# Four pieces of 272 tokens instead of 384 + 352 + 352 in the up-projection of a feed-forward part

## The chip, the core and the metric
The kernel runs on one core of one Trainium2 chip. The metric is device time in microseconds (us) of one execution. The engines are TensorE (PE for its matmuls and PEld for its weight loads in the rows), VectorE (DVE), ScalarE (ACT), GpSimd (POOL) and SyncE (SP, which issues DMAs here). Each runs its own queue in order, and they meet at semaphores only.

## What is computed
One layer of a decoder trunk for 1024 prompt tokens and 8 samples of 8 tokens, 1088 tokens in all. The layer is a three-branch mixer, then a feed-forward part with a causal convolution of width 3 between its two projections, then a final norm. The change lies in the feed-forward part:

```python
x = x + merged @ w_out
u = rmsnorm(x, norm_ffn) @ w_up                      # 1024 -> 2 * 2816 columns
ext = jnp.concatenate([conv_buf.astype(dt), u], axis=1)
c = conv_b + sum(conv_w[i] * ext[:, i:i + T] for i in range(CONV_WIDTH))
gate, val = jnp.split(c, 2, axis=-1)
x = x + (jax.nn.silu(gate) * val) @ w_down
...
y_prompt = rmsnorm(xp, norm_final)
```

## The kernel before
`stage_out_ffn` is the last stage. Activations lie with features on the 128 partitions and the 1088 tokens along the free axis. The work is a list of 92 **units**, numbered n. A unit is one block of 128 output features for all tokens: 8 units "out" (the mixer's output projection), then four parts of the feed-forward part. Each part has "up" units, two for each of its blocks of 128 gated features (h = 0 the gate, h = 1 the value), and then 8 "down" units that add the part's share to x. The parts have 12, 12, 12 and 8 up units, 44 in all; the last part has its down units twice, for two groups of tokens. So the kind of unit goes from up to down four times and from down to up three times, always at an even n.

The matmuls keep more precision than one pass gives: weights and activations are each split into a high and a low half, and every product is three matmuls, low half of x by high weights (L135), high by high (L136), high by low (L137). Each matmul loads its own 128 x 128 weights. A unit runs over its pieces of tokens (`CH`, 384 + 352 + 352), and within a piece over the 8 blocks k of the contraction. So an up unit is 3 pieces x 8 x 3 = 72 matmuls, and 1088 x 24 columns stream through the array.

A piece takes one PSUM bank of 512 fp32 numbers. Of the eight banks even units take 0 to 2 and odd ones 3 to 5; banks 6 and 7 serve sums over partitions (`sums`, L2615) and transposes. PE starts unit n when its weights are split (`ws`) and unit n - 2 has been read out of PSUM (`ev` at least n - 1), which `ready` says. Per unit the others do this:

- SP loads the weights of the unit into the one buffer fu_wt once the previous ones are split.
- VectorE, when unit n's matmuls are done, reads the bank out (L2849 with the norm's factor for an up unit, in pieces of 384, 352 and 288 and then the 64 sample tokens in L2850; L2783 for out and down units), makes the high half of the weights of unit n + 2 (fu_wh, L124), and for an up unit does the convolution (L2857, L2860, L2863) and, after h = 1, the gating (L2867, L2870).
- GpSimd makes the low half of the weights (fu_wl, L129), which releases PE and SP, and the low half of the gated activations (fu_al, L129). ScalarE does the sigmoid and the high half fu_ah.

The first two down units of a part are interleaved: both go over all but the last block of the contraction, since that block's activations come late, and then each does its last block, waiting for `al`. The third down unit needs weights that VectorE only starts after the first has been read out.

The first up unit (n = 8) takes its input while it is still being made: ScalarE writes the high half mh and VectorE the low half ml in 3 x 8 steps (L2790), piece by piece of `CH`, and PE waits before each (piece, k) for that step (`xl`). Behind unit 8 PE does `sums`. VectorE turns them into a mean (L2797, `mean` goes to 3), ScalarE takes the root, and VectorE the reciprocal (L2799). Only then can it read out unit 8, and only after that make the weights of unit 10.

Of the kernel before, what the change touches and what calls it, by code (L numbers as in the profile page):

```python
# [24 lines left out]
KT = D // P  # L25
SEQ, NB, NQ = 1024, 8, 8
TS = NB * NQ
# [20 lines left out]
CH = ((0, 384), (384, 352), (736, 352))  # L48
# [83 lines left out]
def product(nc, out, w, x, start, stop):  # L132

    (wh, wl), (xh, xl) = ((t.bitcast(F32R) for t in pair) for pair in (w, x))
    nc.tensor.matmul(out, wh, xl, start=start, stop=False)  # L135
    nc.tensor.matmul(out, wh, xh, start=False, stop=False)  # L136
    return nc.tensor.matmul(out, wl, xh, start=False, stop=stop)  # L137
# [20 lines left out]
def build(nc, a, outs, scratch):  # L158

    with ExitStack() as ctx:  # L160
# [16 lines left out]
        with tensor("o", [P, 6, T]) as g.branches:  # L177
# [29 lines left out]
            with tensor("mh", [P, KT, T]) as mh, tensor("ml", [P, KT, T]) as ml:  # L207
                with semaphores(g):
                    stage_merge(g, mh, ml)
                with tensor("x1", [P, KT, T]) as x1:  # L210
                    with semaphores(g):
                        stage_out_ffn(g, mh, ml, x1)
# [2239 lines left out]
def stage_out_ffn(g, mh, ml, x1):  # L2452
# [4 lines left out]
    nc, a, V_ = g.nc, g.a, g.nc.vector  # L2457
# [4 lines left out]
    samp = lambda t, o: t[:, S0:EXT].rearrange("p (b q) -> p b q", q=NQ + 2)[:, :, o:o + NQ]  # L2462
# [5 lines left out]
    u, cv = work[:, 0:2, :], work[:, 2:4, :]  # L2468
# [5 lines left out]
    L = len(parts) - 1  # L2474
    units = [("out", 0, t, 0) for t in range(KT)]
# [8 lines left out]
    GROUPS = (((0, 384), (384, 384)), ((768, 320),))  # L2484
    cols = (slice(0, 768), slice(768, T))
    blocks = (range(0, 6), range(6, NJ))
    chunks = lambda n: GROUPS[units[n][3]] if units[n][:2] == ("down", L) else CH

    with ExitStack() as ctx:
        sb = lambda name, shape, dt=F32: ctx.enter_context(nc.sbuf_tensor(f"fu_{name}", shape, dt))  # L2490
# [2 lines left out]
        wl, wh = sb("wl", [P, 2, KT, P]), sb("wh", [P, 2, KT, P])  # L2493
# [13 lines left out]
        s = {n: g.sem(f"fu_{n}") for n in names}  # L2507
# [11 lines left out]
        with nc.Block() as block:  # L2519
# [61 lines left out]
            def _(eng):  # L2581
                def dense(n, c, c0, m, ks, xh, xl, first, last):
                    for k in ks:
                        mm = product(nc, g.ps[:, 3 * (n % 2) + c, 0:m], (wh[:, n % 2, k, :], wl[:, n % 2, k, :]),
                                     (xh[:, k, c0:c0 + m], xl[:, k, c0:c0 + m]), first and k == ks[0], last and k == ks[-1])
                    return mm

                def ready(n):
                    eng.wait_ge(s["ws"], n + 1)
                    if n >= 2:  # L2590
                        eng.wait_ge(s["ev"], n - 1)

                def full(n):
                    ready(n)
                    for c, (c0, m) in enumerate(CH):
                        for k in range(KT):
                            if n == KT:
                                eng.wait_ge(s["xl"], KT * c + k + 1)
                            mm = dense(n, c, c0, m, [k], mh, ml, k == 0, k == KT - 1)
                    mm.then_inc(s["mm"], 1)  # L2600

                def down(n, ks, first, last):
                    for k in ks:
                        eng.wait_ge(s["al"], parts[units[n][1]][0] + k + 1)
                        for c, (c0, m) in enumerate(chunks(n)):
                            mm = dense(n, c, c0, m, [k], ah, al, first and k == 0, last and k == ks[-1])
                    if last:
                        mm.then_inc(s["mm"], 1)
# [44 lines left out]
                for n, (kind, i, t, h) in enumerate(units):  # L2653
                    if kind != "down":
                        full(n)
                        if n == KT:
                            sums()
                        continue
                    nj = parts[i][1]
                    if t == 0 and h == 0:  # L2660
                        ready(n)
                        down(n, range(nj - 1), True, False)
                        ready(n + 1)
                        down(n + 1, range(nj - 1), True, False)
                        down(n, [nj - 1], False, True)
                        down(n + 1, [nj - 1], False, True)
                    elif t >= 2 or h:
                        ready(n)
                        down(n, range(nj), True, True)
# [102 lines left out]
            def _(eng):  # L2772
                def weights(n):
                    if n < NUM:
                        eng.wait_ge(s["w"], 16 * (n + 1))
                        if n >= 2:
                            eng.wait_ge(s["mm"], n - 1)
                        high(eng, wh[:, n % 2, 0:width(n)], wt[:, 0:width(n)]).then_inc(s["wh"], 1)
# [62 lines left out]
                def up(n, i, j, h):  # L2841
                    eng.wait_ge(s["mm"], n + 1)
                    if j:
                        eng.wait_ge(s["co"], 2 * j + h - 1)
                        eng.wait_ge(s["m"] if h == 0 else s["cv"], j if h == 0 else 2 * j)
                    b0 = 3 * (n % 2)
                    for c, (c0, m) in enumerate(CH):
                        m = min(m, SEQ - c0)
                        V_.tensor_tensor(u[:, h, 2 + c0:2 + c0 + m], g.ps[:, b0 + c, 0:m], inv[:, c0:c0 + m], ALU.mult)  # L2849
                    V_.tensor_tensor(samp(u[:, h], 2), g.ps[:, b0 + 2, m:m + TS].rearrange("p (b q) -> p b q", q=NQ),  # L2850
                                     inv[:, SEQ:T].rearrange("p (b q) -> p b q", q=NQ), ALU.mult).then_inc(s["ev"], 1)
                    weights(n + 2)
                    eng.wait_ge(s["ev"], n + 1)
                    eng.wait_ge(s["st"], 2 * j + h + 1)
                    if j:
                        eng.wait_ge(s["act"] if h == 0 else s["al"], j)
                    V_.tensor_scalar(cv[:, h, 0:E], u[:, h, 0:E], column(g.cw[:, 0], h, j), column(g.cb, h, j),  # L2857
                                     ALU.mult, ALU.add).then_inc(s["t0"], 1)
                    eng.wait_ge(s["t0"], 2 * j + h + 1)
                    V_.scalar_tensor_tensor(out=cv[:, h, 0:E], in0=u[:, h, 1:1 + E], scalar=column(g.cw[:, 1], h, j),  # L2860
                                            in1=cv[:, h, 0:E], op0=ALU.mult, op1=ALU.add).then_inc(s["t1"], 1)
                    eng.wait_ge(s["t1"], 2 * j + h + 1)
                    V_.scalar_tensor_tensor(out=cv[:, h, 0:E], in0=u[:, h, 2:2 + E], scalar=column(g.cw[:, 2], h, j),  # L2863
                                            in1=cv[:, h, 0:E], op0=ALU.mult, op1=ALU.add).then_inc(s["cv"], 1)
                    if h:
                        eng.wait_ge(s["sg"], j + 1)
                        V_.tensor_tensor(cv[:, 0, 0:E], sg, cv[:, 0, 0:E], ALU.mult).then_inc(s["m"], 1)  # L2867
                        eng.wait_ge(s["m"], j + 1)
                        eng.wait_ge(s["cv"], 2 * j + 2)
                        V_.tensor_tensor(act[:, 0:E], cv[:, 0, 0:E], act[:, 0:E], ALU.mult).then_inc(s["act"], 1)  # L2870
# [4 lines left out]
                for n, (kind, i, t, h) in enumerate(units):  # L2875
                    if kind == "out":
                        eng.wait_ge(s_i[next(i for i, (k0, k1) in enumerate(KEPT) if k0 <= t < k1)], 16)
                        add(n, t)
                        weights(n + 2)
                        if t == KT - 1:  # L2880
                            for c in range(3):
                                split(c)
                    elif kind == "up":
                        if n == KT:
                            factor()
                        up(n, i, t, h)
                    else:
                        add(n, t)
                        weights(n + 2)
                        if i == L and h == 0 and t >= 2:  # L2890
                            turned(t - 2, 0)
                        if i == L and h == 1:
                            turned(*((KT - 2 + t, 0) if t < 2 else (t - 2, 1)))
                            if t == 4:
                                means(0)
                            if t == 5:
                                scaled(0)
# [48 lines left out]
```

## Time and profile before

| | us |
|---|---|
| median of 3 runs | 2522.24 |
| lowest and highest run | 2520.16, 2529.35 |
| span of the profiled execution | 2527.7 |
| PE busy in it | 2267.6 (90%) |
| VectorE busy in it | 1183.5 (47%) |
| GpSimd busy in it | 665.3 (26%) |

The span runs from the first to the last instruction of the one profiled execution; it is 5.5 us longer than the median, and within the range of the runs. The stage `stage_out_ffn` takes about the last 970 us of it, from 1558 us on, and the first up unit starts at 1667 us. Busy shares of PE are rough, because matmuls overlap in the pipeline and their ends are modelled; what counts is the distance from the start of one matmul to that of the next.

### The profile page before, as it was taken

How to read it: one execution, taken by the hardware profiler on the slowest of the kernel's cores; microseconds unless marked ns; L12 is line 12 of the kernel's file. 1: busy time of each engine (PE TensorE's matmuls, PEld its weight loads, DVE VectorE, ACT ScalarE, POOL GpSimd, SP SyncE). 2: the span in 40 equal slices, each digit the busy share in tenths (PEclk: the TensorE clock that was granted, in tenths of full speed). 3: DMA queues.
4: the chain of work that ended last, by engine and by line, in shares of the span. 5: the costliest groups of instructions: out<-in, count | busy, mean ns of one | idle time of the engine just before them, and what ended most of it. 6: DMA issues, size and time to landing. Idle time of an engine off the chain costs nothing. (4 is left out here: it accounts for less than half of the span.)

```text
span 2527.7 us, 45456 instructions
## 1 busy us (share of the span) xinstructions
PE 2267.6 (90%) x19175; PEld 2062.3 (82%) x19175; DVE 1183.5 (47%) x1734; ACT 454.0 (18%) x704; POOL 665.3 (26%) x607
## 2 busy tenths in 40 slices
PE   4999999999989996777778697989999999999985
PEld 3999999999979884445447555989999999999975
DVE  2332332232134334977765344167726734762743
ACT  4000112231112113742125100121000000000022
POOL 3211111111110000554420012333323323332433
PEclk6999999999999997998988798999999999999998
DMA  6112222222210004959996164111111111111113
GB/s 164 47 49 69 85 88 78 95 88 93 78 46 4 4 5 146 325 166 338 336 315 227 62 200 155 45 34 51 36 49 51 40 38 48 51 34 51 42 47 106
DMA packets 252310, 251.92 MB, mean 100 GB/s; under 512 B 22748, under 2 KB 231365, under 8 KB 250428
## 3 DMA queue, kind: packets, MB, share of 16 engines
q1 hardware_dynamic: 213264, 177.32, 22.7%
q10 hardware_dynamic: 31484, 51.60, 5.9%
q0 software_dynamic: 7360, 20.10, 2.4%
q8 instruction: 152, 2.49, 0.4%
q14 instruction: 50, 0.41, 0.1%
HBM read 210.65 MB, written 60.13 MB: 107 GB/s over the span
## 5 line engine op out<-in xcount | busy, mean ns | idle before, releaser
L135 PE MATMUL ps<-ml,fu_wh 128*128 128x352 f32 (+1 forms) x1248 | 409.8, 328 | 22.5 <-POOL fu_wl L129 17.4
L137 PE MATMUL ps<-mh,fu_wl 128*128 128x352 f32 (+1 forms) x1248 | 408.9, 328 | 0.0
L136 PE MATMUL ps<-mh,fu_wh 128*128 128x352 f32 (+1 forms) x1248 | 408.6, 327 | 0.0
L135 PE MATMUL ps<-xl_a,ap_wh 128*128 128x352 f32 (+2 forms) x1200 | 398.6, 332 | 9.5 <-POOL ap_wl L129 9.5
L136 PE MATMUL ps<-xh_a,ap_wh 128*128 128x352 f32 (+2 forms) x1200 | 396.1, 330 | 0.0
L137 PE MATMUL ps<-xh_a,ap_wl 128*128 128x352 f32 (+2 forms) x1200 | 395.4, 330 | 0.0
L700 DVE TENSOR_TENSOR ap_raw<-ps,inv 128x384 f32<-128x384 f32 x150 | 71.1, 530 | 444.1 <-PE ps L137 444.1
L129 POOL TENSOR_TENSOR fu_wl<-fu_wt,fu_wh 128x1024 fp32r<-128x1024 f32 (+2 forms) x92 | 201.5, 2190 | 263.5 <-DVE fu_wh L124 263.5
L129 POOL TENSOR_TENSOR ap_wl<-ap_wt,ap_wh 128x1024 fp32r<-128x1024 f32 x50 | 119.9, 2398 | 514.7 <-DVE ap_wh L124 514.7
L135 PEld LDWEIGHTS ps<-ml,fu_wh 128*128 128x128 f32 x1248 | 235.7, 189 | 23.7 <-POOL fu_wl L129 23.7
L135 PEld LDWEIGHTS ps<-xl_a,ap_wh 128*128 128x128 f32 x1200 | 227.1, 189 | 16.1 <-POOL ap_wl L129 9.9
L136 PEld LDWEIGHTS ps<-mh,fu_wh 128*128 128x128 f32 x1248 | 236.4, 189 | 0.0
L137 PEld LDWEIGHTS ps<-mh,fu_wl 128*128 128x128 f32 x1248 | 235.3, 189 | 0.0
L136 PEld LDWEIGHTS ps<-xh_a,ap_wh 128*128 128x128 f32 x1200 | 226.8, 189 | 0.7 <-issue 0.7
L137 PEld LDWEIGHTS ps<-xh_a,ap_wl 128*128 128x128 f32 x1200 | 227.0, 189 | 0.0
L135 PE MATMUL ps<-fu_al,fu_wh 128*128 128x384 f32 (+1 forms) x528 | 176.9, 335 | 16.9 <-POOL fu_wl L129 11.6
L137 PE MATMUL ps<-fu_ah,fu_wl 128*128 128x384 f32 (+1 forms) x528 | 175.2, 332 | 0.0
L2783 DVE TENSOR_TENSOR x<-x,ps 128x352 f32<-128x352 f32 (+2 forms) x120 | 57.2, 526 | 251.9 <-PE ps L137 251.9
L136 PE MATMUL ps<-fu_ah,fu_wh 128*128 128x384 f32 (+1 forms) x528 | 174.5, 331 | 0.0
L2849 DVE TENSOR_TENSOR o<-ps,inv 128x384 f32<-128x384 f32 x132 | 59.5, 506 | 128.2 <-PE ps L137 128.2
L135 PEld LDWEIGHTS ps<-fu_al,fu_wh 128*128 128x128 f32 x528 | 101.1, 192 | 19.2 <-POOL fu_wl L129 13.4
L1672 PEld LDWEIGHTS ps<-cf,bs_pk 128*128 128x128 f32 x512 | 62.7, 154 | 62.4 <-DMA bs_pk<-in_cache_sb_k 46.9
(450 smaller groups left out, 3510.6 us busy)
## 6 DMA issues: line engine op xcount, KB each, us to landing
ap_wt<-in_w_in SPq DMA_DIRECT2D x50, 512.0 KB, 3.9
fu_wt<-in_w_up SPq DMA_DIRECT2D x44, 512.0 KB, 3.8
scr_pj<-ap_raw ACTq DMA_DIRECT2D x39, 544.0 KB, 2.7
bs_pk<-in_cache_sb_k SPq DMA_DIRECT2D x130, 128.0 KB, 6.7
out_win_sample<-in_cache_win SPq DMA_DIRECT2D x8, 2040.0 KB, 38.2
bs_pv<-in_cache_sb_v SPq DMA_DIRECT2D x121, 128.0 KB, 6.2
mg_gate<-scr_pj SPq DMA_DIRECT2D x24, 544.0 KB, 3.7
bs_pv<-in_cache_sb_v POOLq DMA_DIRECT2D x75, 128.0 KB, 5.9
```

The lines of the kernel that those rows point to most:

```text
L129: return eng.tensor_tensor(dst.bitcast(F32R), x, xh, ALU.subtract)
L135: nc.tensor.matmul(out, wh, xl, start=start, stop=False)
L136: nc.tensor.matmul(out, wh, xh, start=False, stop=False)
L137: return nc.tensor.matmul(out, wl, xh, start=False, stop=stop)
L700: ins = V_.tensor_tensor(raw[:, t % 2, 1 + c0:1 + c0 + n], g.ps[:, 3 * (t % 2) + c, 0:n], g.inv[:, c0:c0 + n], ALU.mult)
L1672: mm = nc.tensor.transpose(g.ps[:, 2 * (i % 2) + p, k * P:(k + 1) * P], pk[:, n % RK, i, k, p * P:(p + 1) * P], g.ident)
L2783: ins = V_.tensor_tensor(x1[:, t, c0:c0 + m], x1[:, t, c0:c0 + m], g.ps[:, 3 * (n % 2) + c, 0:m], ALU.add)
L2849: V_.tensor_tensor(u[:, h, 2 + c0:2 + c0 + m], g.ps[:, b0 + c, 0:m], inv[:, c0:c0 + m], ALU.mult)
```

## The change
Every up unit goes over four pieces of 272 tokens instead of three. It takes four banks, 0 to 3 for even n and 4 to 7 for odd n; out and down units keep three pieces (or those of the last part) and their banks. Because the banks of the two kinds overlap, two waits are added on PE: the first unit of another kind than the one before waits until that one has been read out (`ev` at least n instead of n - 1), and unit 9, whose banks are now 4 to 7, waits until VectorE has read the sums out of banks 6 and 7. Unit 8's waits for the split input are still by the pieces of `CH`: piece 2 waits for the third piece's steps, and so does piece 3, whose steps are then there. VectorE reads out an up unit in pieces of 272, 272, 272 and 208, and the 64 sample tokens.

```diff
     GROUPS = (((0, 384), (384, 384)), ((768, 320),))
...
-    chunks = lambda n: GROUPS[units[n][3]] if units[n][:2] == ("down", L) else CH
+    QUARTERS = tuple((272 * c, 272) for c in range(4))
+    chunks = lambda n: GROUPS[units[n][3]] if units[n][:2] == ("down", L) else QUARTERS if units[n][0] == "up" else CH
+    bank = lambda n: (4 if units[n][0] == "up" else 3) * (n % 2)
+    switch = lambda n: n and units[n][0] != units[n - 1][0]
...
-                        mm = product(nc, g.ps[:, 3 * (n % 2) + c, 0:m], (wh[:, n % 2, k, :], wl[:, n % 2, k, :]),
+                        mm = product(nc, g.ps[:, bank(n) + c, 0:m], (wh[:, n % 2, k, :], wl[:, n % 2, k, :]),
...
                 def ready(n):
                     eng.wait_ge(s["ws"], n + 1)
                     if n >= 2:
-                        eng.wait_ge(s["ev"], n - 1)
+                        eng.wait_ge(s["ev"], n if switch(n) else n - 1)
 
                 def full(n):
                     ready(n)
-                    for c, (c0, m) in enumerate(CH):
+                    if n == KT + 1:
+                        eng.wait_ge(s["mean"], 3)
+                    for c, (c0, m) in enumerate(chunks(n)):
                         for k in range(KT):
                             if n == KT:
-                                eng.wait_ge(s["xl"], KT * c + k + 1)
+                                eng.wait_ge(s["xl"], KT * min(c, 2) + k + 1)
...
-                    b0 = 3 * (n % 2)
-                    for c, (c0, m) in enumerate(CH):
+                    b0 = bank(n)
+                    for c, (c0, m) in enumerate(QUARTERS):
                         m = min(m, SEQ - c0)
                         V_.tensor_tensor(u[:, h, 2 + c0:2 + c0 + m], g.ps[:, b0 + c, 0:m], inv[:, c0:c0 + m], ALU.mult)
-                    V_.tensor_tensor(samp(u[:, h], 2), g.ps[:, b0 + 2, m:m + TS].rearrange("p (b q) -> p b q", q=NQ),
+                    V_.tensor_tensor(samp(u[:, h], 2), g.ps[:, b0 + 3, m:m + TS].rearrange("p (b q) -> p b q", q=NQ),
```

No instruction changes its place against the others. On VectorE an up unit is, before, in the queue from the reciprocal on (o is one workspace that holds the up-projected rows and the convolution's):

```order
971 L2799 RECIPROCAL inv<-inv 128x1088
972 L2849 TENSOR_TENSOR o<-ps,inv 128x384
973 L2849 TENSOR_TENSOR o<-ps,inv 128x352
974 L2849 TENSOR_TENSOR o<-ps,inv 128x288
975 L2850 TENSOR_TENSOR o<-ps,inv 128x8x8
976 L124 CAST fu_wh<-fu_wt 128x1024
977 L2857 TENSOR_SCALAR o<-o,cw,par 128x1104
```

and now, with the lines of the changed kernel:

```order
971 L2804 RECIPROCAL inv<-inv 128x1088
972 L2854 TENSOR_TENSOR o<-ps,inv 128x272 x3
973 L2854 TENSOR_TENSOR o<-ps,inv 128x208
974 L2855 TENSOR_TENSOR o<-ps,inv 128x8x8
975 L124 CAST fu_wh<-fu_wt 128x1024
976 L2862 TENSOR_SCALAR o<-o,cw,par 128x1104
```

One read more stands between the end of a unit's matmuls and the weights of the next but one.

## Rows read from the trace of the kernel before
**Rows 1.** The page: span, busy time by engine; 40 slices with busy tenths, clock.

```profile
span 2527.7 us, 45456 instructions
...
PE 2267.6 (90%) x19175; PEld 2062.3 (82%) x19175; DVE 1183.5 (47%) x1734; ACT 454.0 (18%) x704; POOL 665.3 (26%) x607
...
PEclk6999999999999997998988798999999999999998
```

**Rows 2.** Stretch of up units: busy time by engine (x instructions), PEclk, DMA share, GB/s.

```profile
1700.00:1815.00 115.00, 115.00 (x701) 115.00 (x700) 90.50 (x90) 12.62 (x16) 47.18 (x50) 1.00 0.16 45
```

**Rows 3.** PE's timeline (start us, us, engine line op tiles): one up unit.

```profile
1756.72 0.34 PE L135 MATMUL ps<-ml,fu_wh 128*128 128x384 f32 x1
...
1760.91 0.32 PE L135 MATMUL ps<-ml,fu_wh 128*128 128x352 f32 x1
...
1768.58 0.34 PE L135 MATMUL ps<-ml,fu_wh 128*128 128x384 f32 x1
```

**Rows 4.** PE's timeline: 320, 256 (two bursts), 128 and 512 columns elsewhere.

```profile
2492.29 0.31 PE L137 MATMUL ps<-fu_ah,fu_wl 128*128 128x320 f32 x1
...
2493.61 0.31 PE L137 MATMUL ps<-fu_ah,fu_wl 128*128 128x320 f32 x1
...
1028.46 0.28 PE L1450 MATMUL ps<-bq_spl,bq_tri 128*128 128x256 f32 x1
...
1028.70 0.28 PE L1450 MATMUL ps<-bq_spl,bq_tri 128*128 128x256 f32 x1
...
1066.40 0.28 PE L1450 MATMUL ps<-bq_spl,bq_tri 128*128 128x256 f32 x1
...
1066.63 0.28 PE L1450 MATMUL ps<-bq_spl,bq_tri 128*128 128x256 f32 x1
...
1024.76 0.27 PE L1450 MATMUL ps<-bq_spl,bq_tri 128*128 128x128 f32 x1
...
1024.98 0.28 PE L1450 MATMUL ps<-bq_spl,bq_tri 128*128 128x128 f32 x1
...
1100.78 0.40 PE L1450 MATMUL ps<-bq_spl,bq_tri 128*128 128x512 f32 x1
...
1101.25 0.40 PE L1450 MATMUL ps<-bq_spl,bq_tri 128*128 128x512 f32 x1
```

**Rows 5.** Timelines of PE and DVE at the first change from up to down.

```profile
1816.02 0.34 PE L135 MATMUL ps<-fu_al,fu_wh 128*128 128x384 f32 x1
...
1816.22 1.35 DVE L2849 TENSOR_TENSOR o<-ps,inv 128x384 f32<-128x384 f32 x3 [4.01 <-PE ps L137]
1817.49 0.21 DVE L2850 TENSOR_TENSOR o<-ps,inv 128x64 f32<-128x64 f32 x1
```

**Rows 6.** Timelines of POOL and PE at the third down unit of that part.

```profile
1834.55 1.80 POOL L129 TENSOR_TENSOR fu_wl<-fu_wt,fu_wh 128x768 fp32r<-128x768 f32 x1 [5.20 <-DVE fu_wh L124]
...
1836.41 0.44 PE L135 MATMUL ps<-fu_al,fu_wh 128*128 128x384 f32 x1 [2.38 <-POOL fu_wl L129]
...
1837.05 0.32 PE L135 MATMUL ps<-fu_al,fu_wh 128*128 128x352 f32 x1
```

**Rows 7.** Timelines of PE and DVE at the first change from down to up.

```profile
1890.05 0.33 PE L135 MATMUL ps<-ml,fu_wh 128*128 128x384 f32 x1
...
1890.25 1.42 DVE L2783 TENSOR_TENSOR x<-x,ps 128x384 f32<-128x384 f32 x3 [6.90 <-PE ps L137]
...
1894.21 0.32 PE L135 MATMUL ps<-ml,fu_wh 128*128 128x352 f32 x1
```

**Rows 8.** PE's timeline in the last part, before the last block's activations.

```profile
2426.17 0.34 PE L137 MATMUL ps<-fu_ah,fu_wl 128*128 128x384 f32 x1
2431.79 0.69 PE L135 MATMUL ps<-fu_al,fu_wh 128*128 128x384 f32 x1 [5.28 <-POOL fu_al L129]
```

**Rows 9.** Timelines of DVE and PE around unit 8, the sums and unit 10.

```profile
1664.38 16.26 DVE L2790 SCALAR_TENSOR_TENSOR ml<-x,par,mh 128x384 fp32r<-128x384 f32 x24
...
1681.32 2.24 PE L2615 MATMUL ps<-o,cf 128*128 128x512 f32 x6
...
1683.24 0.82 DVE L2797 TENSOR_SCALAR inv<-ps 128x512 f32<-128x512 f32 x2 [0.17 <-PE ps L2615]
1685.24 6.95 DVE L2799 RECIPROCAL inv<-inv 128x1088 f32<-128x1088 f32 x1 [1.18 <-ACT inv L2747]
...
1697.34 0.44 PE L135 MATMUL ps<-ml,fu_wh 128*128 128x384 f32 x1 [1.89 <-POOL fu_wl L129]
```

**Rows 10.** Short stretches: busy time by engine, PEclk, DMA share, GB/s.

```profile
1833.80:1837.00 3.20, 0.82 (x5) 0.59 (x4) 1.99 (x5) 0.00 (x0) 1.80 (x1) 1.00 0.00 0
...
2054.00:2057.40 3.40, 3.40 (x14) 3.40 (x13) 0.56 (x1) 0.00 (x0) 0.63 (x1) 0.50 0.37 109
2429.50:2436.30 6.80, 4.51 (x15) 4.19 (x16) 1.62 (x4) 0.84 (x1) 2.98 (x3) 0.50 0.17 64
```

**Rows 11.** Waits from 1700 to 2425: who waited for whom, us, times, longest.

```profile
DVE o L2849 <- PE ps L137: 128.2, 40, 9.8
...
PE ps L135 <- POOL fu_wl L129: 7.8, 4, 2.4
```

## Prediction

> **What bounds the kernel now.** The page comes first: PE is busy in 90% of the span, and over the last stage its digits are 9 nearly throughout, with the granted clock at 9 too, which is 2.4 GHz with short breaks [rows 1]. A busy share of a pipelined engine proves little, so the next view is a stretch of up units alone: in 115 us PE is busy for all 115, at full clock, VectorE for 90.50, GpSimd for 47.18 [rows 2]. The waits say the same from the other side: VectorE's readout waited 128.2 us for PE's matmuls, while PE waited for GpSimd's weights in four places only, 7.8 us together [rows 11]. So up units are bound by PE's issue of matmuls. What counts is the distance between two starts and, wherever PE is made to wait, all that follows it. Little slack can swallow a delay: each part's third down unit waits about 2.4 us for weights [rows 6, 11], but these are begun only after the first down unit has been read out, so that wait moves with PE. Only the wait for the last part's activations, 5.28 us [rows 8], hangs on a chain that starts at the end of the up units.
>
> **Steady up units.** A unit now takes 1768.58 - 1756.72 = 11.86 us. Its first piece takes 4.19 us for 24 matmuls, 0.1746 us each, the other two 7.67 us for 48, 0.1598 each [rows 3]. The change makes 96 matmuls of 72, and streams the same 24 x 1088 columns. So all hangs on the part of a matmul's time that does not shrink with its columns. At 2.4 GHz, 384 columns are 0.160 and 352 are 0.1467 us, so 14.6 and 13.1 ns stand above the pure stream. No row shows 272 columns, but rows on both sides do, with the same kind of operands and a weight load each [rows 4]: 320 columns take 1.32 us for 9, 0.1467 each; 256 columns 0.24 and 0.23 us for two, 0.1175 on average; 512 columns 0.47 us for two, 0.235. A line through 256 and 512 has 0.459 ns a column and almost no constant. Between 256 and 320, the nearest rows, 272 comes to 0.1175 + 16/64 x 0.0292 = 0.1248 us; I take 0.125. Then 96 x 0.125 = 12.00 us. VectorE's readout disturbs the first matmuls of a unit: the piece of 384 behind a change from down to up takes 1894.21 - 1890.05 = 4.16 us [rows 7], one within the stream 4.19. I add these 0.03: 12.03 us, 0.17 more than now.
>
> The bounds: if time were quite proportional to columns, as 384 and 352 are to each other within 0.1%, 272 would take 0.1236 us and the unit 11.90 (+0.04). If 14.6 ns were fixed, it would be 0.1133 + 0.0146 = 0.1279 and 12.31 (+0.45). Of the 44 up units, units 8 and 9 go by other terms (below), which leaves 42: **+7.1 us**, between +1.7 and +18.9.
>
> The Trainium skill, in TensorE: Matmul & The Clock Gate, section Back-to-back issue gap, gives the gap of matmuls as columns / 2.4 GHz and 2.5 ns. By it a unit would go from 24 x 162.5 + 48 x 149.2 ns = 11.06 to 96 x 115.8 ns = 11.12 us, +0.06, and this term would be +2.5 us. Its level is refuted here, 11.06 against 11.86 measured [rows 3]; that the constant is small is what the line through the rows says too.
>
> **Changes from up to down.** Four times PE now waits for the readout of the last up unit before the first down unit. The banks of the two do not even meet (an odd up unit has 4 to 7, an even down unit 0 to 2), but the wait is there. In the trace PE goes on at 1816.02, while the readout runs from 1816.22 until 1817.49 + 0.21 = 1817.70 [rows 5]. One piece more costs about 0.05 us (the whole readout is five instructions for four, and the 64 tokens alone take 0.21). From the end of a releasing instruction to PE's start are 1836.41 - (1834.55 + 1.80) = 0.06 us, and the first three matmuls after a wait then take 0.64 us in place of three times about 0.175, so 0.1 is lost again [rows 6]. Sum: 1817.75 + 0.16 - 1816.02 = 1.89 us. Nothing behind takes it back in the first three parts, as said of the third down unit. In the last part the 5.28 us of waiting for activations [rows 8] take it up, since their chain starts at the same matmul; only the longer readout stays, 0.05. Together **3 x 1.89 + 0.05 = 5.7 us**. Queued behind the waiting matmul are PE's own; SP's weight load and GpSimd's splitting of the next weights hang on VectorE, which goes on.
>
> **Changes from down to up.** Three times PE waits for the last down unit's readout, and here bank 3 is shared. PE goes on at 1890.05, the readout ends at 1890.25 + 1.42 = 1891.67 [rows 7]; with 0.16 as above that is 1.78 us. Before, this readout was covered by the next up unit; now nothing covers it. **3 x 1.78 = 5.3 us.**
>
> **Units 8 and 9.** Unit 8 follows VectorE's 24 steps, which end at 1664.38 + 16.26 = 1680.64, and the sums start at 1681.32, right behind its last three matmuls [rows 9]. After the change two pieces need the last eight steps. The piece at 544 ends no sooner than three matmuls behind the last step, 1680.64 + 0.4 = 1681.04, and then the last piece, 24 x 0.125 = 3.0 us, has nothing left to hide under: the sums start at 1684.04, 2.7 later. From the sums on a chain leads through mean, root, reciprocal (6.95 us), readout of unit 8 and weights to unit 10 at 1697.34, 16.02 us behind [rows 9]; it moves by 2.7 and 0.05. PE's new wait of unit 9 for the mean ends at 1684.04 + (1683.24 + 0.82 - 1681.32) = 1686.78; with 0.16 and 12.03 us unit 9 ends at 1698.97, before the 1700.1 of unit 10's weights. So unit 9's wait and its longer time are hidden, and the term is **+2.75 us**.
>
> **VectorE** gets 44 instructions of some 0.05 us more. With 90.50 of 115 us busy [rows 2], that is covered by its waits for PE. If it were not, it would cost 2 us.
>
> **Clock.** A gap of 2.4 us left the clock at full in one part, a like one in another was followed by 3.40 us at half, and the wait of 5.28 us by 6.80 us at half [rows 10]. The six new waits are shorter, 1.8 us, and in the last part a wait of 5.28 shrinks to some 3.5. I take nothing, with 2 us to either side.
>
> **The sum** is 7.1 + 5.7 + 5.3 + 2.75 = 20.9 us. The profiled execution would go from a span of 2527.7 to 2548.6; it is 5.5 us above the median, and added to the median of 2522.24 the sum gives **2543 us**, 0.8% slower. With the bounds of the pitch it is 2522.2 + 15.5 = 2538 to 2522.2 + 32.7 = 2555.
>
> **The rivals.**
> (a) *The waits at the changes of kind cost nothing*, because the delay is taken up by a later wait, or the readout is done sooner than I think. Then 7.1 + 2.75 + 0.05 us are left, 2532 us. Against it: each readout starts only when PE would already go on [rows 5, 7].
> (b) *Faster: short pieces stream at the bare 2.4 GHz.* The surplus of 13 to 15 ns would belong to long pieces alone, and 272 columns would take 0.1133 us: a unit of 10.88 + 0.03 = 10.91 us, -0.95, times 42 is -40 us; with +13.8 from the waits 2496 us. It decides from a pitch of (11.86 - 0.03 - 13.8/42)/96 = 0.1198 us: below that the change is faster than before. Against it: 256 columns, shorter still, already take 0.1175, 11 ns above their stream of 0.1067 [rows 4]. The Trainium skill's page named above would have 2.5 ns on top of the stream at any length, which in this rival's place gives 11.15 us a unit and 2506 us.
> (c) *The weight load becomes the bound.* 128 columns take (1024.98 - 1024.76)/2 = 0.11 us [rows 4], about twice their stream of 0.053, so a load cannot be had for less than that. If in a long stream load and matmul hinder each other as they come close (0.11 against 0.113), the pitch could rise to the chord between 128 and 320 columns, 0.110 + 144/192 x 0.0367 = 0.1375 us; a unit is then 13.23, +1.37, and the time 2522.2 + 57.5 + 13.8 = 2594. For it: the 256-column bursts are only three or four matmuls long. Against it: these very bursts have a load each and lie on the line of the long pieces.
> (d) *The clock falls at each new wait.* Then 3.4 us at half after each of six, as in rows 10, cost 1.7 us each: 10 more, 2553 us.
>
> **Chances.** My forecast with its bounds of the pitch 0.80; (a) 0.07; (b) 0.03; (c) 0.04; (d) 0.06. The range should leave out (b), (c) and the outer ends: 2532 to 2557. A measurement of this kernel tells about 0.5% from no change, so slower by over 0.5% begins at 2534.9 us. (a) lies mostly within it, and of the forecast a small share at the proportional end: faster 0.03, within 0.5% 0.12, slower 0.85.
>
> **What would show it.** In the profile of the changed kernel the start of an up unit is 12.0 us from the next one's (11.90 to 12.31), and matmuls of 128x272 are 0.125 us apart; PE waits seven times for VectorE's readout, six of them 1.6 to 1.9 us and the last before a wait for fu_al that is 1.8 us shorter than 5.28; the sums start 3.4 us behind the last step of L2790 instead of 0.7. A pitch below 0.120 or above 0.130, or readout waits that another wait gives back, would make the prediction wrong.

## Result: 0.8% slower

| | median, us | lowest to highest |
|---|---|---|
| before (5 runs) | 2524.03 | 2520.16 to 2531.14 |
| changed (5 runs) | 2543.59 | 2542.39 to 2549.23 |

The ratio is 1.0079, with a 95% interval of 1.0058 to 1.0101. The prediction was 2543 us. The profiled executions differ by as much: a span of 2547.0 us against 2527.7.

The page of the changed kernel: span and busy time by engine, two groups of instructions (busy us, mean ns of one | idle time before), and the clock over 40 slices.

```profile
span 2547.0 us, 47612 instructions
...
PE 2283.2 (90%) x20231; PEld 2076.3 (82%) x20231; DVE 1185.4 (47%) x1778; ACT 454.2 (18%) x704; POOL 666.7 (26%) x607
...
PEclk6999999999999997998988798999999999999998
...
L135 PE MATMUL ps<-ml,fu_wh 128*128 128x272 f32 (+2 forms) x1600 | 471.6, 295 | 27.3 <-POOL fu_wl L129 16.1
...
L2854 DVE TENSOR_TENSOR o<-ps,inv 128x272 f32<-128x272 f32 (+1 forms) x176 | 62.4, 418 | 143.6 <-PE ps L137 143.6
```

PE has 1056 matmuls more (44 x 24), VectorE 44 instructions more for 1.9 us more of busy time. VectorE's readouts wait 143.6 us for PE where they waited 128.2 [rows 11]: VectorE is still not the bound.

PE's timeline, one up unit in the stream, by the first matmul of each of its four pieces and of the next unit (start us, duration us, engine line op tiles). It answers to [rows 3].

```profile
1733.60 0.28 PE L135 MATMUL ps<-ml,fu_wh 128*128 128x272 f32 x1
...
1736.61 0.28 PE L135 MATMUL ps<-ml,fu_wh 128*128 128x272 f32 x1
...
1739.63 0.29 PE L135 MATMUL ps<-ml,fu_wh 128*128 128x272 f32 x1
...
1742.66 0.28 PE L135 MATMUL ps<-ml,fu_wh 128*128 128x272 f32 x1
...
1745.63 0.28 PE L135 MATMUL ps<-ml,fu_wh 128*128 128x272 f32 x1
```

The unit takes 12.03 us instead of 11.86, its pieces 3.01, 3.02, 3.03 and 2.97; many others take 12.05. Over the 38 units that follow one another without a wait, a matmul takes 0.1255 us on average, with 0.1235 in the last piece.

The first change from up to down and the first from down to up, PE and VectorE (they answer to [rows 5, 7]); in brackets the idle time ahead and who ended it.

```profile
1817.66 0.28 PE L137 MATMUL ps<-mh,fu_wl 128*128 128x272 f32 x1
1819.64 0.41 PE L135 MATMUL ps<-fu_al,fu_wh 128*128 128x384 f32 x1 [1.69 <-issue]
...
1817.99 1.42 DVE L2854 TENSOR_TENSOR o<-ps,inv 128x272 f32<-128x272 f32 x4 [4.24 <-PE ps L137]
1819.32 0.22 DVE L2855 TENSOR_TENSOR o<-ps,inv 128x64 f32<-128x64 f32 x1
...
1894.92 0.32 PE L137 MATMUL ps<-fu_ah,fu_wl 128*128 128x352 f32 x1
1896.84 0.36 PE L135 MATMUL ps<-ml,fu_wh 128*128 128x272 f32 x1 [1.60 <-DVE x L2788]
```

At the first PE starts 1.98 us after its last matmul, where a matmul of 272 columns in a stream is followed by the next after 0.12, and in step with the end of the readout at 1819.54; at the second 1.92 instead of 0.16. All four changes of the first kind and all three of the second are like these within 0.01 us.

Units 8 and 9 and the wait for the last part's activations (they answer to [rows 9, 8]).

```profile
1661.54 16.26 DVE L2795 SCALAR_TENSOR_TENSOR ml<-x,par,mh 128x384 fp32r<-128x384 f32 x24
...
1681.30 2.24 PE L2620 MATMUL ps<-o,cf 128*128 128x512 f32 x6
1684.18 0.36 PE L135 MATMUL ps<-ml,fu_wh 128*128 128x272 f32 x1 [0.65 <-DVE inv L2802]
...
1697.40 0.39 PE L135 MATMUL ps<-ml,fu_wh 128*128 128x272 f32 x1 [0.94 <-POOL fu_wl L129]
...
2447.38 0.34 PE L137 MATMUL ps<-fu_ah,fu_wl 128*128 128x384 f32 x1
2452.13 0.69 PE L135 MATMUL ps<-fu_al,fu_wh 128*128 128x384 f32 x1 [4.41 <-POOL fu_al L129]
```

The sums start 3.5 us behind the last step of the input (1677.80) where it was 0.7. From the starts of PE's first matmuls at unit 8, unit 10 and each change of kind, the 19.3 us between the two spans fall out so:

| stretch of PE | before, us | changed, us | difference | forecast |
|---|---|---|---|---|
| units 8 and 9 | 30.05 | 32.96 | +2.9 | +2.75 |
| units 10 to 51, without the waits | 498.1 | 506.0 | +7.9 | +7.1 |
| three waits from up to down, 1.85 each | | | +5.5 | +5.7 |
| three waits from down to up, 1.75 each | | | +5.3 | +5.3 |
| three stretches of down units, without the waits | 223.7 | 225.2 | +1.5 | 0 |
| from the last part's first down unit to the end, with the fourth wait | 108.6 | 107.6 | -1.0 | 0 |
| all ahead of unit 8, which the change doesn't touch | 1667.3 | 1664.5 | -2.8 | |

The rows from unit 8 on add up to 22.1 us, where 20.9 were forecast. The 2.8 us less ahead of unit 8 lie between two executions of the same code, and nothing ties the 1.0 us less at the end to the change. The runs of the kernel before lie up to 11 us apart, so that the median came within 0.6 us of the forecast is in part chance.

### The profile page after: what moved, and what is told of

Read it like the earlier page. It is cut to its first block and busy times, and to the rows that moved or that the text cites. A ratio compares the mean times of both kernels' runs of the same rounds, so it can differ in the third digit from the quotient of the medians.

```text
span 2547.0 us, 47612 instructions
## 1 busy us (share of the span) xinstructions
PE 2283.2 (90%) x20231; PEld 2076.3 (82%) x20231; DVE 1185.4 (47%) x1778; ACT 454.2 (18%) x704; POOL 666.7 (26%) x607
## 5 line engine op out<-in xcount | busy, mean ns | idle before, releaser
L135 PE MATMUL ps<-ml,fu_wh 128*128 128x272 f32 (+2 forms) x1600 | 471.6, 295 | 27.3 <-POOL fu_wl L129 16.1
L137 PE MATMUL ps<-mh,fu_wl 128*128 128x272 f32 (+2 forms) x1600 | 470.7, 294 | 0.0
L136 PE MATMUL ps<-mh,fu_wh 128*128 128x272 f32 (+2 forms) x1600 | 470.7, 294 | 0.0
L135 PEld LDWEIGHTS ps<-ml,fu_wh 128*128 128x128 f32 x1600 | 303.2, 189 | 29.9 <-POOL fu_wl L129 22.2
L136 PEld LDWEIGHTS ps<-mh,fu_wh 128*128 128x128 f32 x1600 | 303.3, 190 | 0.0
L137 PEld LDWEIGHTS ps<-mh,fu_wl 128*128 128x128 f32 x1600 | 302.9, 189 | 0.0
L2854 DVE TENSOR_TENSOR o<-ps,inv 128x272 f32<-128x272 f32 (+1 forms) x176 | 62.4, 418 | 143.6 <-PE ps L137 143.6
```

## Experiments

### The waits, taken away and put in alone
Two theories stood against each other from the start: that each wait costs its readout, since what waits later moves along with PE, and rival (a), that a later wait gives it back. Three kernels settle it. The first leaves the wait out at the changes to down units, whose banks do not meet those of the last up unit:

```diff
-                        eng.wait_ge(s["ev"], n if switch(n) else n - 1)
+                        eng.wait_ge(s["ev"], n if switch(n) and units[n][0] == "up" else n - 1)
```

> The changed kernel, with the added wait kept only where the first up unit follows a down or out unit; at the four changes from up to down PE goes on as before. My theory (each added wait costs its readout, 1.85 us, and nothing gives it back in the first three parts): the four gaps of 1.97 us at these changes close to 0.13, the last of them is given back before the last block's activations anyway, so the stage is 3 x 1.85 = 5.6 us shorter than the changed kernel and about 1.0057 times before. Rival (a later wait takes the delay up, or the clock moves instead): the gaps close and the time of the stage stays within 2 us of the changed kernel.

Measured: 2541.76 us, 1.0053 times before (1.0034 to 1.0071). The gaps close to 0.12 us, and from the first matmul of the stage to the end it takes 978.9 us against 984.8: 6.0 less, where 5.6 was expected. The medians, 2541.76 us here and 2543.59 for the changed kernel, are too close to tell the two apart; it is the traces that do.

The second lays the banks so that no wait at a change is needed:

```diff
-    bank = lambda n: (4 if units[n][0] == "up" else 3) * (n % 2)
+    bank = lambda n: (3 if units[n][:2] == ("down", L) else 4) * (n % 2)
...
-                        eng.wait_ge(s["ev"], n if switch(n) else n - 1)
+                        eng.wait_ge(s["ev"], n - 1)
...
-                        ins = V_.tensor_tensor(x1[:, t, c0:c0 + m], x1[:, t, c0:c0 + m], g.ps[:, 3 * (n % 2) + c, 0:m], ALU.add)
+                        ins = V_.tensor_tensor(x1[:, t, c0:c0 + m], x1[:, t, c0:c0 + m], g.ps[:, bank(n) + c, 0:m], ALU.add)
```

> The changed kernel with all units but the last part's down units in banks 0 to 3 and 4 to 7, so that none of the waits at changes of kind is needed and none is made; unit 9's wait for the mean stays. My theory: 3 x 1.85 + 3 x 1.77 = 10.9 us shorter than the changed kernel; what is left against before is the shape of the pieces, 42 x 0.18 = 7.6 us, and 2.9 us at units 8 and 9: 1.0042 times before. Rival (the waits cost nothing, pieces all): no difference to the changed kernel, 1.0079.

Measured: 2535.55 us, 1.0044 (1.0029 to 1.0058), where 1.0042 was expected. The stage takes 973.0 us, 11.9 less than in the changed kernel; 10.9 were expected, and the clock differs too (see Clock, below). PE goes from down to up as before the change:

```profile
1889.28 0.33 PE L137 MATMUL ps<-fu_ah,fu_wl 128*128 128x352 f32 x1
1889.45 0.28 PE L135 MATMUL ps<-ml,fu_wh 128*128 128x272 f32 x1
```

The third is the kernel before with its three pieces and only the waits:

```diff
+    switch = lambda n: n and units[n][0] != units[n - 1][0]
...
-                        eng.wait_ge(s["ev"], n - 1)
+                        eng.wait_ge(s["ev"], n if switch(n) else n - 1)
```

> The kernel before, pieces of 384 + 352 + 352, with only the waits at changes of kind added. My theory: 3 x 1.79 + 3 x 1.76 = 10.7 us slower than before, 1.0042; unit distance stays 11.86 us. Rival (the cost is in the pieces alone): 1.000.

Measured: 2536.99 us, 1.0050 (1.0032 to 1.0069); a unit stays at 11.86 us. Its stage is 13.1 us longer than before, 2 to 3 more than expected, because the clock fell to half in two more parts (see Clock, below). PE's timeline shows both kinds of wait:

```profile
1810.48 0.32 PE L137 MATMUL ps<-mh,fu_wl 128*128 128x352 f32 x1
1812.43 0.41 PE L135 MATMUL ps<-fu_al,fu_wh 128*128 128x384 f32 x1 [1.62 <-issue]
...
1887.91 0.32 PE L137 MATMUL ps<-fu_ah,fu_wl 128*128 128x352 f32 x1
1889.83 0.41 PE L135 MATMUL ps<-ml,fu_wh 128*128 128x384 f32 x1 [1.60 <-DVE x L2784]
```

So the waits cost what their readouts last, alone as well as with the pieces, and rival (a) falls. They are about half of the loss, 10.8 of the 22.1 us from unit 8 on, and none of them was needed: the second kernel does without.

### What a matmul costs over its stream
Is it the number of matmuls that costs, or their lengths? Three pieces of other sizes keep the number at 72 and change the lengths:

```diff
+    PIECES = ((0, 512), (512, 320), (832, 256))
+    chunks = lambda n: GROUPS[units[n][3]] if units[n][:2] == ("down", L) else PIECES if units[n][0] == "up" else CH
...
-                                eng.wait_ge(s["xl"], KT * c + k + 1)
+                                eng.wait_ge(s["xl"], KT * min(c + 1, 2) + k + 1)
```

> The kernel before with up units in three pieces of 512 + 320 + 256: 72 matmuls and 3 banks as before, no wait added. Theory A (a matmul takes a fixed surplus over its stream, so it is their number, 96 for 72, that cost 0.17 us a unit): the number is as before, a unit takes 11.86 us again. Theory B (the surplus goes with the columns, 0.459 ns a column at these lengths, and 384 and 352 happen to lie 1% below): 24 x (0.235 + 0.1467 + 0.1175) = 11.98 us, +0.12 a unit, in spite of the same number. Unit 8 has a first piece that needs the second group of steps; some 1 to 2 us more there. Time: A 1.0005, B 1.0025.

Measured: 2530.27 us, 1.0021 (1.0009 to 1.0033). PE's timeline, the starts of the three pieces and of the next unit:

```profile
1925.45 0.40 PE L135 MATMUL ps<-ml,fu_wh 128*128 128x512 f32 x1
...
1930.92 0.30 PE L135 MATMUL ps<-ml,fu_wh 128*128 128x320 f32 x1
...
1934.43 0.28 PE L135 MATMUL ps<-ml,fu_wh 128*128 128x256 f32 x1
...
1937.31 0.40 PE L135 MATMUL ps<-ml,fu_wh 128*128 128x512 f32 x1
```

The unit takes 11.86 us again: theory A holds and B falls. Its matmuls take 0.228, 0.146 and 0.120 us, which is 14.6, 12.9 and 13.3 ns over 512, 320 and 256 columns at 2.4 GHz. Most of what is lost against before is at unit 8, whose first piece needs the second group of steps from its start: PE waits 11.18 us there and not 5.12, and from the stage's first matmul to the start of unit 9 are 6.6 us more, where 1 to 2 were expected. Another 2.9 are in the stretches of down units, where the clock fell to half in three parts and not in one.

Four pieces that are not equal, on the second kernel's banks and with unit 8 left in its three pieces, try the same sum on 96 matmuls. The kernel with four of 272 under the same conditions stands beside it:

```diff
-    QUARTERS = tuple((272 * c, 272) for c in range(4))
+    QUARTERS = ((0, 256), (256, 320), (576, 256), (832, 256))
```

> The same with pieces of 256 + 320 + 256 + 256 in place of four of 272: 96 matmuls again, the same columns, other starts. Theory A (fixed 13.3 ns a matmul, as 256, 320 and 512 show in the stream, and 272's mean of 12.2 is a matter of where its pieces start): 96 x 13.3 ns + 10.88 = 12.16 us a unit. Theory D (the cost is the number of matmuls and nothing else): 12.04 as with 272.

Measured: 2543.02 us, 1.0075 (1.0048 to 1.0101), and a unit of 12.16 us, as theory A says to the last digit, so D falls. The time is 8 us above that of the kernel beside it. The longer unit explains 42 x 0.11 = 4.6 of them, and in the profiled executions the clock fell to half behind the third down unit's wait in three parts here and in one there. PE's timeline, the four pieces and the next unit:

```profile
1929.01 0.28 PE L135 MATMUL ps<-ml,fu_wh 128*128 128x256 f32 x1
...
1931.89 0.31 PE L135 MATMUL ps<-ml,fu_wh 128*128 128x320 f32 x1
...
1935.41 0.28 PE L135 MATMUL ps<-ml,fu_wh 128*128 128x256 f32 x1
...
1938.29 0.28 PE L135 MATMUL ps<-ml,fu_wh 128*128 128x256 f32 x1
...
1941.17 0.28 PE L135 MATMUL ps<-ml,fu_wh 128*128 128x256 f32 x1
```

The kernel beside it differs from the one without waits at the changes by unit 8 alone:

```diff
-    chunks = lambda n: GROUPS[units[n][3]] if units[n][:2] == ("down", L) else QUARTERS if units[n][0] == "up" else CH
+    chunks = lambda n: GROUPS[units[n][3]] if units[n][:2] == ("down", L) else QUARTERS if units[n][0] == "up" and n != KT else CH
...
-                                eng.wait_ge(s["xl"], KT * min(c, 2) + k + 1)
+                                eng.wait_ge(s["xl"], KT * c + k + 1)
```

> The kernel without waits at changes of kind (the one before in bank layout 0 to 3 and 4 to 7, pieces of 272), and unit 8 in the pieces 384 + 352 + 352, so that only units 9 to 51 have four pieces. My theory: units 8 and 9 take 30.1 us together as in the kernel before, unit distance 12.03 to 12.05, so 42 x 0.18 = 7.7 us over before in the stage, 1.003. Rival (the 2.9 us at units 8 and 9 come from unit 9's wait for the mean, which is still here): they stay near 33 us.

Measured: 2534.95 us, 1.0039 (1.0025 to 1.0052). Units 8 and 9 take 17.11 + 13.16 = 30.27 us, near the 30.05 of before and not the 32.96: the piece that hung over the end of the input cost the 2.7 us, and unit 9's wait for the mean, still there, costs 0.2 at most. The other units take 12.05 us. The stage, 971.3 us, is 8.8 us longer than before, where 7.7 were expected.

Where does the floor lie? Five pieces, two to a bank:

```diff
+    PIECES = tuple((218 * c, min(218, T - 218 * c)) for c in range(5))
...
+                def o(n, c):
+                    return 256 * (c % 2) if units[n][0] == "up" else 0
...
-                        mm = product(nc, g.ps[:, 3 * (n % 2) + c, 0:m], (wh[:, n % 2, k, :], wl[:, n % 2, k, :]),
+                        mm = product(nc, g.ps[:, 3 * (n % 2) + (c // 2 if units[n][0] == "up" else c), o(n, c):o(n, c) + m], (wh[:, n % 2, k, :], wl[:, n % 2, k, :]),
```

> The kernel before with up units in five pieces of 218, 218, 218, 218 and 216 tokens, two to a bank, three banks, no wait added. The run with 512 + 320 + 256 kept 11.86 us a unit, so a matmul seems to cost its stream at 2.4 GHz and a fixed 13 ns. Theory A (that sum alone): 0.0908 + 0.013 = 0.104 us, a unit 120 x 0.104 = 12.5 us. Theory C (a weight load takes 0.110 us and none overlaps another, rival (c) of the prediction with its true threshold): 120 x 0.111 = 13.3 us a unit, +1.46 x 43 = 63 us, 1.025 times before; by A 1.011.

Measured: 2594.34 us, 1.0283 (1.0263 to 1.0304), where theory C had 1.025; units 8 and 9, which it left out, take 5.3 us more than before. A piece takes 2.68 us and a unit 13.40, so 0.1117 us a matmul, where its stream and 13 ns would be 0.104:

```profile
1943.01 0.28 PE L135 MATMUL ps<-ml,fu_wh 128*128 128x218 f32 x1
...
1945.69 0.28 PE L135 MATMUL ps<-ml,fu_wh 128*128 128x218 f32 x1
...
1956.41 0.27 PE L135 MATMUL ps<-ml,fu_wh 128*128 128x218 f32 x1
```

That is the distance of matmuls of 128 columns too [rows 4]. The trace of the kernel before even has it at two columns. In PE's timeline there, 18 such matmuls, each with a load of 128 x 128 weights, take 1.98 us from the start of the first to that of what follows, 0.110 each, at full clock:

```profile
506.19 2.05 PE L500 MATMUL ps<-aux,o 128*128 128x2 f32 x18
508.17 0.44 PE L135 MATMUL ps<-xl_a,ap_wh 128*128 128x384 f32 x1
```

So the floor does not depend on the columns. What is left is the load, or another fixed step of the pair; no run tells these apart. Rival (c) names a real bound, but one that lies below 272 columns: stream and 13.3 ns come to 0.1117 us at some 236 columns, an estimate from the two measured values.

### Why 272 columns take a little less
272 columns take 12.2 ns over the stream on average, with 10.2 in the last piece. Two kernels, from the one with unit 8 in three pieces, turn the banks round and the order of the pieces:

```diff
-                        mm = product(nc, g.ps[:, bank(n) + c, 0:m], (wh[:, n % 2, k, :], wl[:, n % 2, k, :]),
+                        mm = product(nc, g.ps[:, bank(n) + (3 - c if chunks(n) == QUARTERS else c), 0:m], (wh[:, n % 2, k, :], wl[:, n % 2, k, :]),
```

VectorE's readouts take the turned banks too.

> The kernel with four pieces of 272 from unit 9 on and no waits at changes of kind, its pieces' banks turned round (tokens 0 to 271 in the fourth bank). Open is why 272 columns take 12.1 ns over their stream on average where 256, 320 and 512 take 13.3, with 10.2 in the last piece alone. Theory S (where a piece starts among the tokens): the piece of tokens 816 to 1087 stays at 0.1235 us a matmul, the others at 0.1256 to 0.1267. Theory B (its bank): the piece in the fourth bank of the four, now tokens 0 to 271, has the 0.1235.

```diff
-                    for c, (c0, m) in enumerate(chunks(n)):
+                    for c, (c0, m) in list(enumerate(chunks(n)))[::-1 if chunks(n) == QUARTERS else 1]:
```

> The same kernel with its banks as they were, but the pieces of an up unit done in the opposite order, tokens 816 to 1087 first. Theory S (start among the tokens): the piece of tokens 816 to 1087, now first, has 0.1235 us a matmul. Theory T (time within the unit, when VectorE and GpSimd have least to do beside it): the last piece done, now tokens 0 to 271, has it.

Measured, one execution each (2536.00 and 2529.35 us, too few to compare times): with the banks turned the pieces take as before, 0.1256, 0.1265, 0.1266, 0.1235 us a matmul; with the order turned the piece of tokens 816 to 1087, now first, has the 0.1235:

```profile
1918.04 0.29 PE L135 MATMUL ps<-ml,fu_wh 128*128 128x272 f32 x1
...
1921.01 0.29 PE L135 MATMUL ps<-ml,fu_wh 128*128 128x272 f32 x1
...
1924.05 0.29 PE L135 MATMUL ps<-ml,fu_wh 128*128 128x272 f32 x1
```

The 0.1235 goes with the tokens 816 to 1087, not with the bank or the time in the unit: S holds, and B and T fall. The order has a part too, though: the piece of tokens 0 to 271 takes 0.1256 when it is done first and 0.1266 when it is last. The kernel before shows a difference between equal lengths as well. Its second piece of 352, from token 384, takes 0.1608 us a matmul, from 1760.91 [rows 3] to the line below, and its third, from token 736 and up to 1768.58, takes 0.1588:

```profile
1764.77 0.32 PE L135 MATMUL ps<-ml,fu_wh 128*128 128x352 f32 x1
```

It is not the tokens themselves: 256 columns from token 832, nearly the same ones, keep their 13.3 ns. By which rule start and length set the surplus is open.

### A shorter wait elsewhere
The third down unit of a part waits for weights that VectorE makes only after a readout [rows 6]. On the kernel before, the two change places:

```diff
                     else:
-                        add(n, t)
                         weights(n + 2)
+                        add(n, t)
```

> The kernel before, with VectorE making the high half of the weights of unit n + 2 ahead of reading out unit n in down units. The wait of 2.7 us for the third down unit's weights holds a readout of 1.33 us; without it 1.4 us remain, 3 x 1.35 = 4 us less in the first three parts, if PE's wait hangs on this chain. In the last part 14 units wait likewise and could give up to 0.9 us each, unless the weights' transfer is what they wait for. 0.995 to 0.998 times before. Rival (the transfer or the transposes end last there): 0.998 to 1.000.

Measured: 2518.89 us, 0.9981 times before (0.9972 to 0.9991). PE's gap goes from 2.70 to 1.47 us, and each stretch of down units in the first three parts to 72.79, from 74.03 and, in the part where the clock fell, 75.60. The last part gives nothing: most of its gaps are 2.7 us (2.64 before). So the expectation held for the first three parts and its rival for the last, and the ratio lies at the edge between the two. It is the fastest of these kernels, by a little.

```profile
1827.47 0.56 DVE L124 CAST fu_wh<-fu_wt 128x768 fp32r<-128x768 f32 x1 [6.88 <-PE ps L137]
1827.94 1.41 DVE L2783 TENSOR_TENSOR x<-x,ps 128x384 f32<-128x384 f32 x3
```

## Why the prediction was right, point by point
**The bound.** PE bound the up units before and after: PE busy for the whole of 115 us, with VectorE at 91.74 for 90.50 [rows 2]. Its 44 instructions more cost nothing.

```profile
1700.00:1815.00 115.00, 115.00 (x920) 115.00 (x919) 91.74 (x100) 12.69 (x16) 47.79 (x50) 1.00 0.16 45
```

**Steady up units.** The number was right, 7.9 us for 7.1, and the reasoning behind it was not. The prediction laid a line through two-interval bursts and read from it "0.459 ns a column and almost no constant". In an unbroken stream 256 columns take 0.120 us where the bursts had 0.1175, and 512 take 0.228 where they had 0.235. What holds is a constant of some 13.3 ns (12.1 to 14.6 by piece, 13.3 to 13.6 over a whole unit of other pieces than 272). With it 272 columns would be 0.1267 us, a unit 12.16, and the term 13 us. Where the pieces of 272 start happens to save 1.1 ns a matmul, 0.11 us a unit, which brought it back to the value from the bursts: two errors that met. The upper bound, a fixed surplus, was the right mechanism; it was set too high by 384's 14.6 ns. That 384 and 352 looked proportional is chance as well: the 13.1 ns of 352 are the mean of 14.2 and 12.1 in two pieces.

The Trainium skill (TensorE: Matmul & The Clock Gate, Back-to-back issue gap) has a fixed 2.5 ns above the stream. It calls this the gap of a matmul by itself and says that in a stream of loads and matmuls both set the distance, which the prediction left out. That a surplus is fixed, within 2 ns, is what the runs with 512 + 320 + 256 and with 256 + 320 + 256 + 256 show; for these matmuls, each with a load of its own, it is 13.3 and not 2.5, and the 24 more in a unit cost 0.3 us, not 0.06, if nothing is gained by their starts.

**The waits.** Both were right within 0.1 us each: the gaps are 1.85 and 1.75 us longer, from the readout, its one piece more (0.07 us for the 0.05 forecast) and the restart, and the first matmuls behind them are slower (12.12 us for the unit in place of 12.05; that share stands with the up units in the table). That nothing gives them back in the first three parts was right as well. In the last part the step "a wait of 5.28 shrinks to some 3.5" failed in its place, not in its sum: it shrank to 4.41, because a short wait for weights ahead of it, which made a distance of 1.00 us between two matmuls, is gone and had already given back 0.83. In PE's timeline of the kernel before:

```profile
2423.09 0.44 PE L135 MATMUL ps<-fu_al,fu_wh 128*128 128x384 f32 x1 [0.66 <-POOL fu_wl L129]
```

It is the fourth of the four waits, 7.8 us together, in [rows 11], of which the prediction followed up only the three of 2.4; the total of the part was unharmed.

**Units 8 and 9.** 2.9 us for 2.75; the cause, the last piece behind the end of the input, is shown by the kernel that leaves unit 8 in three pieces.

**Clock.** Taken at nothing with 2 us to either side. The stretches of down units came 1.5 us longer, 1.3 by the clock and 0.2 by the slower matmuls behind the new waits. After the third down unit's wait of 2.4 us the clock fell to half (1.2 GHz) in two parts here, in one before:

```profile
1839.70:1843.10 3.40, 3.02 (x10) 3.02 (x11) 0.00 (x0) 0.00 (x0) 0.33 (x1) 0.50 0.42 116
2065.00:2068.40 3.40, 3.40 (x13) 3.40 (x12) 0.56 (x1) 0.00 (x0) 0.55 (x1) 0.50 0.43 112
```

No new wait of 1.8 us at a change of kind was followed by a fall in any kernel, which rules out rival (d). But the old wait is a draw: in the profiled executions it was followed by one in three parts of three with 512 + 320 + 256, in none with the banks laid anew, in 19 of 33 over the eleven kernels that have it, and each costs 1.4 to 1.6 us. With the wait shortened to 1.47 us no part had one. Whether that is the reason or chance, three parts of one execution cannot say. Nor is a wait as short as the new ones, 1.6 to 1.7 us idle, safe everywhere: in the last part, where short matmuls and short waits lie close together, the clock fell right behind a wait of 1.64 us in the kernel with unit 8 in three pieces (PE's timeline, then a stretch with PEclk):

```profile
2451.84 0.41 PE L2635 MATMUL ps<-cf,x 128*128 128x128 f32 x2 [1.64 <-DVE x L2813]
...
2452.40:2455.80 3.40, 3.40 (x13) 3.40 (x12) 0.31 (x1) 0.00 (x0) 1.59 (x2) 0.50 0.26 77
```

**Rival (b)**, the bare stream, needed a pitch below 0.120 us at 272 columns. It was 0.1255, and even 256 columns stand at 0.120, 13.3 ns above their stream.

## What to carry to other kernels
In a stream where each matmul loads its own weights, cost a split by the number of matmuls first (here 13.3 ns each over the stream, and never under some 0.11 us with 128 x 128 weights), and take the surplus from an unbroken stream, not from bursts of a few. When a tile takes more banks, look at which waits the new layout really needs: about half of this loss came from waits that another assignment of the same eight banks makes needless. And where an engine paces itself on an input that is still being made, let only one piece of its work need the last piece of that input. Here two did, and the second, 3 us long, had nothing left to hide under.

## What the runs showed of the hardware
- Matmuls with 128 x 128 weights of their own, fp32r operands, in unbroken streams: the stream at 2.4 GHz and 12.1 to 14.6 ns at 256, 320, 352, 384 and 512 columns; a floor of 0.1117 us at 218 columns. Two columns with a 128 x 128 load have 0.110.
- The surplus of a piece of 272 columns depends on where it starts: 10.2 ns from token 816, whatever the bank and the order; 12.3 to 13.5 from 0, 272 and 544, where the order moved the one from 0 by 1 ns.
- After a wait of 2.4 us between full streams the granted clock fell to half in 19 of 33 places, and in some parts and not in others of the same execution. After the 17 new waits at changes of kind, 1.6 to 1.7 us idle, it never did, but among the short matmuls of the last part it did after 1.64 us.
